# Sample attention of a one-core layer: three sequences in flight, a value step behind each key bank

## The reference, cut to what matters

```python
def nsa_sample(q, kv, cw, cache, page_table, win):
    past = cache[page_table].reshape(DB, past_len, N_KV_KINDS, N_KV_HEADS, HEAD_DIM)
    full = jnp.concatenate([past, kv_rows.astype(past.dtype)], axis=1)
    o_cmp, o_slc = nsa_global(q, full[:, :, 0], full[:, :, 1], full[:, :, 2], full[:, :, 3], q_pos, cw, False)
    wk = jnp.concatenate([win, jnp.stack([k_win, v_win], axis=2)], axis=1)
    o_win = local_attend(q, wk[:, :, 0], wk[:, :, 1], (diff >= 0) & (diff < WINDOW))
```

## Time and profile before

| | |
|---|---|
| median of 3 runs | 3213.75 us (3211.16 to 3216.8) |
| profiled execution, its own time | 3218.59 us |
| its span, first to last instruction | 3216.9 us |
| TensorE busy | 3084.0 us (96%) |
| VectorE, ScalarE busy | 1528.2 us, 1184.5 us |
| sample stage, first product to last output | 1742.0 to 2033.7 us |

### The profile page before, as it was taken

How to read it: one execution, slowest core, us unless ns; L and a number is a source line. 1 busy time by engine, 2 the same in 40 slices (tenths; PEclk the granted TensorE clock), 3 DMA queues, 4 the chain that set the end, 5 groups by cost and what they waited for, 6 DMA issues and landing times.

```text
span 3216.9 us, 59558 instructions
## 1 busy us (share of the span) xinstructions
PE 3084.0 (96%) x22622; PEld 2843.8 (88%) x22622; DVE 1528.2 (48%) x2587; ACT 1184.5 (37%) x1768; POOL 431.7 (13%) x568
## 2 busy tenths in 40 slices
PE   7999999999999999999997888899799999999998
PEld 6888888899999999999995555799799999999998
DVE  5333335455453333333764555555544444444455
ACT  5333334232322333333773333333343333333443
POOL 5444442001010110001001223000000000000000
PEclk9999999999999999999998999899899999999999
DMA  8766665668787876654325889554344444544543
GB/s 260 258 188 212 191 213 175 219 211 272 249 288 241 287 250 201 207 177 143 119 68 170 293 303 343 192 187 153 95 148 157 145 146 152 154 146 143 157 140 103
DMA packets 429382, 623.88 MB, mean 194 GB/s; under 512 B 14359, under 2 KB 358360, under 8 KB 428016
## 3 DMA queue, kind: packets, MB, share of 16 engines
q1 hardware_dynamic: 372690, 411.16, 40.1%
q0 software_dynamic: 55696, 210.54, 19.7%
q10 hardware_dynamic: 864, 0.34, 0.0%
HBM read 603.26 MB, written 35.25 MB: 198 GB/s over the span
## 4 chain that ended last, share of the span: by engine, by line
PE 92%; DVE 3%; DMA 2%; issue 1%; ACT 1%; SPq 1%; POOLq 0%; POOL 0%; DVEq 0%; ACTq 0%
PE bank L1425 22%; PE bank L1427 21%; PE bank L1426 21%; PE bank L1352 4%; PE bank L1350 4%; PE bank L1351 4%; PE bank L1293 3%; PE bank L1381 2%; PE bank L1613 2%; PE bank L1661 1%; PE bank L1621 1%; PE bank L1314 1%; PE bank L1652 1%; PE bank L1570 1%; DMA sb_raw<-in_w_in 1%
## 5 line engine op out<-in xcount | busy, mean ns | idle before, releaser
L1956 DVE TENSOR_TENSOR sb_w_lo<-sb_raw,sb_w_hi 128x1024 fp32r<-128x1024 f32 x592 | 724.2, 1224 | 682.3 <-ACT sb_w_hi L956 654.9
L1425 PE MATMUL bank<-sb_act_hi,sb_w_hi 128*128 128x320 f32 x3200 | 1002.2, 313 | 23.7 <-DVE sb_act_lo L1983 14.0
L1427 PE MATMUL bank<-sb_act_lo,sb_w_hi 128*128 128x320 f32 x3200 | 992.2, 310 | 0.0
L1426 PE MATMUL bank<-sb_act_hi,sb_w_lo 128*128 128x320 f32 x3200 | 992.2, 310 | 0.0
L956 ACT ACTIVATE sb_w_hi<-sb_raw 128x1024 fp32r<-128x1024 f32 x592 | 624.1, 1056 | 854.8 <-PE bank L1427 834.3
L1425 PEld LDWEIGHTS bank<-sb_act_hi,sb_w_hi 128*128 128x128 f32 x3200 | 604.3, 189 | 36.4 <-issue 25.6
L1426 PEld LDWEIGHTS bank<-sb_act_hi,sb_w_lo 128*128 128x128 f32 x3200 | 604.3, 189 | 0.0
L1427 PEld LDWEIGHTS bank<-sb_act_lo,sb_w_hi 128*128 128x128 f32 x3200 | 603.7, 189 | 0.0
L1903 DVE TENSOR_TENSOR sb_keyT_lo<-bank,sb_keyT_hi 128x512 fp32r<-128x512 f32 x256 | 176.6, 691 | 304.6 <-ACT sb_keyT_hi L893 304.4
L1425 PE MATMUL bank<-sb_hid_hi,sb_w_hi 128*128 128x320 f32 x1024 | 317.5, 310 | 0.0
L1427 PE MATMUL bank<-sb_hid_lo,sb_w_hi 128*128 128x320 f32 x1024 | 316.4, 309 | 0.0
(11 more groups left out here) (381 smaller groups left out, 3351.6 us busy)
## 6 DMA issues: line engine op xcount, KB each, us to landing
sb_raw<-in_w_mlp SPq DMA_DIRECT2D x64, 2048.0 KB, 9.0
sb_raw<-in_w_in SPq DMA_DIRECT2D x60, 2048.0 KB, 8.3
sb_ada_half<-in_w_ada POOLq DMA_DIRECT2D x64, 1024.0 KB, 7.9
sb_ada_raw<-in_w_ada SPq DMA_DIRECT2D x16, 2048.0 KB, 12.3
sb_krow<-in_cache_nsa_kv SPq DMA_DIRECT2D x128, 256.0 KB, 4.6
sb_vrow<-in_cache_nsa_kv POOLq DMA_DIRECT2D x128, 256.0 KB, 5.7
sb_raw<-in_w_conv_proj SPq DMA_DIRECT2D x8, 2048.0 KB, 8.3
sb_raw<-in_w_attn_proj SPq DMA_DIRECT2D x8, 2048.0 KB, 8.3
```

The source lines that it names most:

```text
L1425: mm(out, w_hi[:, buf, k, :], x_hi[:, kk, :], start=(kk == 0), stop=False)
L1426: mm(out, w_lo[:, buf, k, :], x_hi[:, kk, :], start=False, stop=False)
L1427: last = mm(out, w_hi[:, buf, k, :], x_lo[:, kk, :], start=False, stop=(kk == KT - 1))
L1956: V.tensor_tensor(w_lo[:, buf], raw[:, (t // 2) % 2, CH * ch:CH * ch + CH, P * (t % 2):P * (t % 2) + P], w_hi[:, buf].bitcast(F32), ALU.su ...
```

## The change

A step now handles three sequences, `step(a, b, n, par, more)` with a = n - 2, and there are ten steps. In steps with all three, values of a (chunk 3, then the new and window values) are multiplied between the head turns of key chunks 0 and 1 of n, and values of b (chunks 0 to 2) between the head turns of chunks 2, 3 and the window. The maximum is taken in four parts behind each chunk's scores (`part_max`) with a small maximum over them at the step's end; the exponentials of the cache rows are four pieces. The new values are no longer turned: POOL requests them for each sequence from the output tensors that earlier stores wrote, behind an added wait for those stores. The mixing of the three outputs of a sequence moves one step later. SP's requests of keys are as they were.

```diff
@@ -451,12 +453,15 @@
 
         def sample_steps(eng, step):
 
-            step(None, 0, 0, True)
-            with eng.Fori(0, NB // 2 - 1) as i:
-                step(i * 2, i * 2 + 1, 1, True)
-                step(i * 2 + 1, i * 2 + 2, 0, True)
-            step(NB - 2, NB - 1, 1, False)
-            step(NB - 1, None, 0, False)
+            step(None, None, 0, 0, True)
+            step(None, 0, 1, 1, True)
+            with eng.Fori(0, NB // 2 - 2) as i:
+                step(i * 2, i * 2 + 1, i * 2 + 2, 0, True)
+                step(i * 2 + 1, i * 2 + 2, i * 2 + 3, 1, True)
+            step(NB - 4, NB - 3, NB - 2, 0, True)
+            step(NB - 3, NB - 2, NB - 1, 1, False)
+            step(NB - 2, NB - 1, None, 0, False)
+            step(NB - 1, None, None, 1, False)
 
 
...
@@ -791,9 +796,12 @@
                                        cache[ds(page, 1), :, 3, :].rearrange("a p n -> p (a n)")).then_inc(s_vd[c], 16)
                 pool.wait_ge(s_spv, b * 5 + 2 * CREDIT)
                 pool.sem_inc(s_pass[2], 1)
+                pool.dma_start(vnew[par][:, 0, :], A["out_kv_sample"][0, ds(b, 1), :, 3].rearrange("a s h d -> (a s) (h d)")).then_inc(s_vn[par], 16)
+                pool.dma_start(vnew[par][:, 1, :], A["out_win_sample"][0, ds(b, 1), WIN - NSTEP:WIN, 1].rearrange("a s h d -> (a s) (h d)")).then_inc(s_vn[par], 16)
                 pool.dma_start(vrow[4][:, :, :], win[ds(b, 1), :, :, 1, :].rearrange("a p c n -> p (a c) n")).then_inc(s_vd[4], 16)
 
             compressed(0, 0)
+            pool.wait_ge(s_rowdma[2], 16 * (3 + 2 + NB))
             values(0, 0, True, chunks=(2, 3))
             values(1, 1, True)
             with pool.Fori(1, NB // 2 - 1) as i:
...
+                def keys_turn(pc, h):
...
+                    if h == 0:
+                        pe.wait_ge(s_kd[slot], n * 128 + 64 * (pc // 2 + 1) if pc < 4 else n * 16 + 16)
+                    pe.wait_ge(s_ktev[h % 2], banks_before(n, pc) + h // 2 + CREDIT)
+                    for k in range(4):
+                        last = tr(bank[h % 2][:, P * k:P * k + P], krow[:, slot, k, P * h:P * h + P], ident[:, :])
+                    last.then_inc(s_ktr, 1)
...
+                def weigh_chunk(q, c, k, drained):
+
+                    if k == 0:
+                        pe.wait_ge(s_ktev[c % 2], prob_banks_before(q, c, drained) + 1 + CREDIT)
+                        pe.wait_ge(s_vd[c], q * 64 + 64)
+                    last = weigh(1, PTs[:, 4 * c + k, :], vrow[c][:, k, :], c == 0 and k == 0, False)
+                    if k == 3:
+                        last.then_inc(s_spv, 1)
+
+                def weigh_rest(q, k, drained):
+
+                    if k == 0:
+                        for f in (4, 5):
+                            pe.wait_ge(s_ktev[f % 2], prob_banks_before(q, f, drained) + 1 + CREDIT)
+                        pe.wait_ge(s_vn[par], q * 16 + (32, 16)[par])
+                        pe.sem_inc(s_pass[1], 1)
+                        weigh(1, PTn[:, 0, :], vnew[par][:, 0, :], False, True)
+                        pe.wait_ge(s_vd[4], q * 16 + 16)
+                    weigh(2, PTs[:, 16 + k, :], vrow[4][:, k, :], k == 0, False)
+                    if k == 3:
+                        weigh(2, PTn[:, 1, :], vnew[par][:, 1, :], False, True).then_inc(s_spv, 1)
 
                 if n is not None:
                     pe.wait_ge(s_new, n * 2 + 2)
...
-                    pe.wait_ge(s_so, n - 1 + CREDIT)
-                    for br in range(2):
-                        for h in range(NKV):
-                            last = tr(bank[6 + br][0:NSTEP, P * h:P * h + P], knew[par][:, 8 * br + 4 + h, :], ident[:, :])
-                    last.then_inc(s_vnt, 1)
-                    keys(0)
-                    keys(1)
+                for k in range(4):
+                    if n is not None:
+                        keys_turn(0, k)
+                    if a is not None:
+                        weigh_chunk(a, 3, k, b is None)
+                for k in range(4):
+                    if n is not None:
+                        keys_turn(1, k)
+                    if a is not None:
+                        weigh_rest(a, k, b is None)
+                if n is not None:
                     pe.wait_ge(s_cexp, n * 2 + 1)
-                    pe.wait_ge(s_vne, n * 2 + 2)
                     tr(bank[7][0:NC_S, 0:P], C_s[:, 0:NC_S], ident[:, :]).then_inc(s_selp, 1)
                     scores(0)
                     pe.wait_ge(s_cexp, n * 2 + 2)
                     mm(bank[7][:, P:P + NSB], PTcs[par][:, :], selw[0:NC_S, :], start=True, stop=True).then_inc(s_selp, 1)
...
                 if b is not None:
                     probs_turn(0)
                     probs_turn(1)
+                if a is not None:
+                    pe.wait_ge(s_os, a * 3 + 3)
+                    pe.wait_ge(s_so, a + CREDIT)
+                    tr(bank[6][:, 0:P], os_row[:, :], ident[:, :]).then_inc(s_sot, 1)
                 if n is not None:
                     pe.wait_ge(s_sel, n * 12 + 5)
                     mm(bank[7][:, 192:192 + NSB], grp[:, :], z_s[:, :], start=True, stop=True).then_inc(s_selp, 1)
...
-                if n is not None:
-                    keys(4)
-                    scores(3)
-                if b is not None:
-                    pe.wait_ge(s_sm, b * 5 + 5)
-                    tr(bank[6][:, 0:P], os_row[:, :], ident[:, :]).then_inc(s_sot, 1)
+                for c in range(3):
+                    for k in range(4):
+                        if n is not None:
+                            keys_turn(2 + c, k)
+                        if b is not None:
+                            weigh_chunk(b, c, k, n is None)
+                    if n is not None:
+                        scores(1 + c)
+                    if b is not None and c < 2:
+                        probs_turn(2 * c + 2)
+                        probs_turn(2 * c + 3)
                 if n is not None:
                     scores(4)
...
+                def part_max(pc):
+
+                    dve.wait_ge(s_sev, n * 5 + pc + 1 + CREDIT)
+                    V.tensor_reduce(nst[:, 12 + pc:13 + pc], S_s[:, 512 * pc:512 * pc + 512 + (NSTEP if pc == 3 else 0)], AX.X, ALU.max).then_inc(s_pm, 1)
...
-                dve.wait_ge(s_sev, b * 5 + 5 + CREDIT)
-                bias(0)
...
-                    for br in range(2):
-                        V.tensor_copy(vnew[par][:, br, :], bank[6 + br][0:NSTEP, :]).then_inc(s_vne, 1)
...
```

More of the change, by code:

```diff
@@ L1600, in _, with sample_pe @@
             pe.wait_ge(s_sel, 1)
-            def sample_pe(b, n, par, more):
-                def keys(pc):
+            def sample_pe(a, b, n, par, more):
+                def keys_turn(pc, h):
                     slot = pc % 2 if pc < 4 else 2
-                    if pc < 4:
-                        pe.wait_ge(s_kd[slot], n * 128 + 64 * (pc // 2 + 1))
-                    else:
-                        pe.wait_ge(s_kd[2], n * 16 + 16)
-                    for h in range(NKV):
-                        pe.wait_ge(s_ktev[h % 2], banks_before(n, pc) + h // 2 + CREDIT)
-                        for k in range(4):
-                            last = tr(bank[h % 2][:, P * k:P * k + P], krow[:, slot, k, P * h:P * h + P], ident[:, :])
-                        last.then_inc(s_ktr, 1)
+                    if h == 0:
[4 more added lines that the diff above has]
+                    last.then_inc(s_ktr, 1)
                 def scores(pc):
@@ new lines, in sample_pe @@
+                if n is not None:
+                    pe.wait_ge(s_new, n * 2 + 2)
+                    pe.wait_ge(s_cd[par], n * 16 + (32, 16)[par])
+                    for keys_of, c0, cn in ([kc_s[:, par, h, :] for h in range(NKV)], 0, NC_S), \
+                            ([knew[par][:, h, :] for h in range(NKV)], P, NSTEP), \
+                            ([knew[par][:, 8 + h, :] for h in range(NKV)], P + NSTEP, NSTEP):
+                        for h in range(NKV):
+                            last = mm(bank[4][32 * h:32 * h + 32, c0:c0 + cn], q_s[par][:, 32 * h:32 * h + 32], keys_of[h], start=True, stop=True)
+                    last.then_inc(s_ssc, 1)
@@ new lines, in sample_pe @@
+                for k in range(4):
+                    if n is not None:
+                        keys_turn(0, k)
+                    if a is not None:
+                        weigh_chunk(a, 3, k, b is None)
+                for k in range(4):
+                    if n is not None:
+                        keys_turn(1, k)
+                    if a is not None:
+                        weigh_rest(a, k, b is None)
+                if n is not None:
+                    pe.wait_ge(s_cexp, n * 2 + 1)
+                    tr(bank[7][0:NC_S, 0:P], C_s[:, 0:NC_S], ident[:, :]).then_inc(s_selp, 1)
+                    scores(0)
+                    pe.wait_ge(s_cexp, n * 2 + 2)
```

(26 more changed lines are left out.)

235 lines of the change are left out of this document (91 added, 144 removed).

## The result

The changed kernel takes 3209.7 us (median of 20 runs, 3202.2 to 3219.0), the kernel before 3216.9 us in the runs beside it (20, 3211.2 to 3225.3): a ratio of 0.9975, 95% interval 0.9966 to 0.9984. It is faster by 7 us, where 31.7 us were forecast and 3202 was the upper end of the range. The profiled execution of the changed kernel, 3202.3 us, is one of the fastest of its 20; against the profiled execution of before it saves 16.3 us, twice what the medians show. The other executions of a kernel left no trace, so what differs between them stays open.

The account below looks back on a forecast made before the run. It took engines and copies as today's bound, then late keys at 29.6 us; with 0.9 for the clock, 30.5 a step. Savings 31.2 + 1.5 - 1.0 = 31.7 us gave 3186.9 profiled, 3182 median, range 3165 to 3202.

Parts of the forecast that it names:

- The chunk with values: Key chunk whose head turns alternate with value pieces on TensorE: 0.68 + 1.43 + 0.68 = 2.8 us.
- the chain of engines: One full step, TensorE to copies and back: middle 15.1, head 11.5, plus 0.35 for selection steps, 27.0 us.
- the keys' bound: Step limited by chunk 2's late key request: 23.5 us plus a landing of 6.1, 29.6 us.
- Request and landing: Chunk 2's keys: 3.8 us to issue four requests, then 6.1 us until the last lands.
- Waits for banks and for `q_s`: TensorE waits 1.34 us for bank 0 after the probabilities' turn, and some 0.9 us for `q_s` in the head.
- Bytes: DMA moves 11.0 MB a step: 29.5 us at 374 GB/s, 28.4 at 388.
- The clock, +0.9 us: TensorE's clock falls after the chunk 2 wait in some steps, costing up to 2.5 us; 0.9 taken per step.
- The clock rival: Clock falls after the chunk 2 wait in every step: step 32.0 to 33.5 us, 3197 mid-range; chance 0.19.
- The first step and the end: First step saves 1.5 us from turned new values; the stage's end loses 1.0 us to later exponentials and window values.
- the wait of about 2 us for chunk 2: Sign expected after the change: chunk 2's head turns wait for DMA, 2 us or so.
- the 2.06 us at L1643: TensorE's wait for copies of new values in each step before, 2.06 us, expected to vanish.
- the DMA share: Sign expected over the steps after the change: DMA share 0.97 or more, at 350 to 370 GB/s.

Follow-up runs that it names:

- the run with four places: The changed kernel with four places for the cache's key chunks in place of two, each chunk requested a step ahead: 3178.7 us, ratio 0.9876.
- values behind: The changed kernel with four key places and each chunk's value products after its sixteen key turns, not between them: 3171.4 us, ratio 0.986.
- in pairs: The changed kernel with four key places and value products issued after every second head turn, two heads' worth at a time: 3172.4 us, ratio 0.9863.

## Why the prediction was wrong

The mechanism was right: keys bound the step, through the wait for chunk 2, at two places. Four terms of the sum were wrong.

**The chunk with values, 2.8 us: the step that failed.** "Two head turns with two value pieces are 1.36 us of TensorE" added 0.43 and 0.25, both taken from stretches in which TensorE did one kind of thing. With a change of tile between them, a pair takes 0.94 and not 0.68, a chunk 3.65. This term stood in both bounds. In the chain of engines it made 27.0 of what the run with four places measures as 29.34: three chunks of the middle alone are 2.6 us, and the middle is where that run has them, 17.5 us for 15.1. In the keys' bound, 15.1 + 0.9 + 0.86 + 2.8 = 19.7 us had four such chunks; with 3.65 it is 23.1, and with 3.8 + 6.1 that is 33.0 us, before any clock. The step shown above has 33.2 (1872.28 to 1905.47 from chunk 2 to chunk 2), the mean 32.49; both hold the clock's share, so the sum's other terms were together 1 to 1.5 us too long.

```profile
1872.28 1.11 PE L1630 MATMUL bank<-sb_ident,sb_krow 128*128 128x128 f32 x4 [1.86 <-DMA sb_krow<-in_cache_nsa_kv]
```

**Request and landing, 3.8 + 6.1.** Right in the step shown: 3.7 and 5.95. Over the seven steps the median landing was 5.6 us and the longest 11.0.

**Waits for banks and for `q_s`.** The turn behind the probabilities comes 1.35 us after them (1.34 was forecast); the wait for `q_s` and `knew` was taken too long, 0.5 us and not 0.9. VectorE was no bound.

**Bytes, 29.5 or 28.4 us.** The rate was near: the run with four places moves 364 GB/s over its steps, those with values behind or in pairs 367 to 371; 374 came from a window that, 34 us long, held the reload of `mx`, too. The 11.0 MB were too many. A step's own requests are 32 of 256 KB and two of 1024 KB, 10.5 MB; most of the rest of the 77 MB is two reloads of 2560 KB each (`ga` and `mx`) that fall into the seven steps once. So the bound was too high, and one run has steps of 28.26 us. In the changed kernel it never came last, since the same transfers asked for earlier fitted into 29.34 us. The figures of the Trainium skill's page "HBM Reference" (section "Specifications (TRN2)" and the text under its table) for one core, 358 and 425 GB/s, enclose what was measured, nearer to the lower.

**The clock, +0.9 us.** This term was right in kind and in size: the clock falls behind the wait for chunk 2, to 0.61 over 4.2 us, which cost that chunk 1.4 us (1905.47 to 1910.52 is 5.05, against 3.65), and it fell in five steps of seven, so 1.0 us a step. Its mean over the steps is 0.96, not under 0.9. The clock rival, at 32.0 to 33.5 us a step, named the step that came, but by luck: of the 2.9 us that the step lies over the 29.6 of the keys' bound, the clock gave 1.0. The rest came by way of a chunk time that the rival had at 2.8 us as well.

**The first step and the end, +1.5 and -1.0.** They were 2.8 and -4.5. At the end I let the window values land in the 8.6 us of the earlier trace rows and set them against the cover they had had. The end now drains one more sequence's values in less time, and SP's 2 MB of weights were requested at 2001.32, 0.1 us ahead of them. That a request's wait condition (two value steps of the last sequence) comes earlier in a changed pipeline was not in the sum.

Of the signs, the wait of about 2 us for chunk 2 came and the 2.06 us at L1643 went; the DMA share (0.96 for 0.97 or more) and the rate (336 GB/s for 350 to 370) did not come.

Together: 7 x (32.49 - 30.5) = 13.9 us too little from the steps, and 2.2 us from the ends, which takes the forecast from 3186.9 to 3203 for a profiled execution; it took 3202.3. For the median the forecast took a further 4.8 us off, the distance of the profiled execution from a median of three runs; in the 20 runs beside the result it is 1.7 us, which explains 3.1 us of the miss. The median of the changed kernel lies 7 us over its profiled execution instead of under it, and why is not explained. The scatter is 17 us for the changed kernel (20 runs) and 11 and 3 us for four places and for four places in pairs (four runs each).

## What to carry to other kernels

Before interleaving two kinds of matmul, measure a stretch in which they alternate; the sum of their times apart leaves out what each change of tile costs, and here that ate all of the cover gained (12.3 us of waits for copies in seven steps became 1.4, and the step was no shorter). When a step is shortened, recompute for each buffer the way from "place free" through issue and landing to use: a buffer count that cost nothing before (ratio 1.000 with four places) cost 31 us after, some 22 of them in the seven steps. And look for requests whose wait counts steps of the stage that was changed, above all large ones of the next stage: they move with it, into the transfers that end it.

## What the runs showed of the hardware

TensorE's change between four 128x128 transposes and eight 32 column products costs about 0.13 us. From the turn's start to the product's it is 0.59 us (1912.84 to 1913.43) where four transposes alone take 0.43, and back 0.35 (1913.43 to 1913.78) where eight products take 0.25. From a value product to the scores, which are 32 columns wide too, it is 0.24 (1916.25 to 1916.49): no price. And a chunk's excess over 2.7 us halves as the changes do (3.65, 3.20 us). The DMA share is a poor gauge of what is left: 0.96 at 336 GB/s in the changed kernel rose to 1.02 at 364 with the same transfers asked for earlier. At 371 GB/s keys took 10.8 us in the median to land, twice the 5.6 of the changed kernel, and delayed nothing, since they were asked for a step ahead.
